# A two-layer streaming encoder on one core: products that nobody reads in three of TensorE's waits, a later wait for the latent projection's weights, and VectorE one tile further ahead

## The chip, the cores and the metric

The kernel runs on one core of one Trainium2 chip. The metric is the device time of one launch in microseconds (us), here the median of three runs. Smaller is better.

A core has TensorE (PE in the profile; its weight loads are PEld), VectorE (DVE), ScalarE (ACT), GpSimd (POOL) and a queue engine that only issues transfers (SP). Each runs its own instruction stream in order and waits for others on semaphores. Matrix products read the on-chip memory and write into PSUM, which is used here as four "pairs" of banks, `psum[0]` to `psum[3]`.

## The reference

Two layers work on 592 tokens (512 new, 16 meta, 64 sampled) of width 1024, in float32. Layer 0 mixes tokens with four recurrent heads and four attention heads, layer 1 with latent attention. Each mixer is followed by a layer norm and a mixture of 16 experts.

```python
for l in range(2):
    y = even_mixer(x) if l == 0 else odd_mixer(x)
    x = layer_norm(ALPHA * x + y)
    f = moe(x)                    # best of 4 groups, top 2 of its 4 experts, weights w
    x = layer_norm(ALPHA * x + f)

def odd_mixer(x):                 # its first steps
    cq, ckv, kpe = split(x @ w_in, [512, 768])      # 832 columns
    cq, ckv = rms_norm(cq), rms_norm(ckv)           # the latents
    kpe = rope(kpe)
    ...                           # queries, keys, values, attention, w_out

def moe(x):
    scores = sigmoid(x @ router_w)                  # 16 columns
    ...                           # choice of two experts per token
    y = sum_over_chosen(w * (silu(x @ w_gate[e]) * (x @ w_up[e])) @ w_down[e])
```

## The kernel before

**Tiles.** The tokens lie in five tiles, four of 128 and one of 80 (`TILES`, `NT = 5`). Token rows are written to memory after each norm, and transposed on TensorE into `xT` for the next product.

**Router and experts, once for each layer.** In `out_and_experts` TensorE makes the output projection of a tile (L1352), and transposes the normed tiles (`normed_tile`, L1072). After the last one it makes the router's logits (`router_logits`: L1192, then L1419). VectorE turns these into the mask of chosen experts in a chain of small operations that ends with `maskb` (L2212). TensorE then counts how many tokens choose each expert (L1366 to L1370, the "rk" product), VectorE writes one-hot rows (L2259), and TensorE reads the tokens of each slot out of them (`slot_tokens`, L1386). From these numbers GpSimd gathers the token rows of the first block of 128 slots. `experts` works through 13 such blocks. For a block TensorE transposes the rows (`rows_t`, L1434), makes gate and up (`gate_up`, L1448), transposes the hidden values (L1457) and makes the down product (`down`, L1469). After the thirteenth block every engine passes a loop over blocks that overflow (L1494 on TensorE), which are none here.

**Between the experts of layer 0 and the latents.** GpSimd gathers each token's two expert rows. On VectorE `combine_tile(i)` weights and adds them to the residual (L2408, L2410), `combined_stats(i)` takes mean and variance and subtracts the mean (L2419 to L2425), and `combined_norm(i)` scales and writes the tile (L2435). The scale itself comes from GpSimd (`scale_row`, L850 and L851). `latents(i)` (L2389 to L2399) norms and rotates what TensorE made of tile i. TensorE's loop over the tiles is: the 512 query columns of tile i (L1545), the transposes of tile i+1 (L1072), the 320 key columns of tile i (L1545), and the transposes of the latents of tile i-1 (`latents_t`, L1532 to L1535). The weights come in two items, `mi0` for the 512 columns and `mi1` for the 320. The queue issues `mi0` during the experts and `mi1` only when the first token rows have been gathered.

**What sets the order** is the code itself: each engine's program is written out by hand, and `claim`, `filled` and `wait_ge` place the waits. `weights(pe, name)` is a wait for an item's transfer. Matrix products are float32, except those on masks and one-hot rows, which are bfloat16. The code passes the identity as the operand to be loaded in some of these; `lev` is a bfloat16 constant of 1024 columns.

Of the kernel before, what the change touches and what calls it, by code (L numbers as in the profile page):

```python
# [25 lines left out]
NT = len(TILES)  # L26
# [120 lines left out]
def build_step(nc, const_where, consts, a, o):  # L147
# [11 lines left out]
    with ctx:  # L159
# [14 lines left out]
        identb = sb("identb", [128, 128], BF16)  # L174
        iotab = sb("iotab", [128, 128], BF16)

        def const(name):
            lo, hi = const_where[name]
            return cst[:, lo:hi] if lo < n_f32 else cstb[:, lo - n_f32:hi - n_f32]
# [4 lines left out]
        lev = const("lev").rearrange("p (l t) -> p l t", l=8)  # L184
# [467 lines left out]
        def weights(pe, name):  # L652

            it = next(x for x in items if x[0] == name)
            pe.wait_ge(*w_in[it[1]][name])
            return it[5]
# [409 lines left out]
        def _(pe):  # L1066
# [271 lines left out]
            def out_and_experts(l):  # L1338
# [19 lines left out]
                normed_tile(l, NT - 1)  # L1358
                router_logits(l, 1)

                pe.wait_ge(*mk_sb[l])
                ps = claim(pe, ("rk", l))
                for i in range(NT):
# [5 lines left out]
                for j in range(NT):  # L1369
                    last = pe.matmul(ps[:, 80:96], const("ones"), maskb[:, NE * j:NE * j + NE],  # L1370
                                     start=(j == 0), stop=(j == NT - 1))
                last.then_inc(pe_full.sem(("rk", l)), 1)

                slot_tokens(l, 0)
                slot_tokens(l, 1)
                pe.wait_ge(*ps_free[("rk", l)])
                pe.wait_ge(*ps_free[("lg", l, 1)])
                pe.wait_ge(*ps_free[("T", 2 * l, 4)])
                experts(l)

            def slot_tokens(l, g):
                ps = claim(pe, ("ix", l, g))
# [139 lines left out]

            out_and_experts(0)

            wq, wkv = weights(pe, "mi0"), weights(pe, "mi1")

            def latents_t(i):
                P = TILES[i]
                pe.wait_ge(*mi_sb[i])
# [4 lines left out]
                    pe.transpose(ps[:, 512 + 128 * k:512 + 128 * k + P], cvb[0:P, i % 2, 128 * k:128 * k + 128], ident[0:P, 0:P])  # L1534
                pe.transpose(ps[:, 768:768 + P], kpb[0:P, i % 2, :], ident[0:P, 0:P]).then_inc(pe_full.sem(("mt", i)), 1)  # L1535

            pe.wait_ge(*r_sb[(1, 0)])
            transpose_tile(1, 0, rb[:, 0, :])
            for i in range(NT):
                P = TILES[i]  # L1540
                pe.wait_ge(*evac[("T", 1, i)])
                ps = claim(pe, ("mi", i))
                for w, lo, n in ((wq, 0, 512), (wkv, 512, 320)):
                    for k in range(KD):
                        last = pe.matmul(ps[0:P, lo:lo + n], xT[:, k, 128 * i:128 * i + P], w[:, k, :],  # L1545
                                         start=(k == 0), stop=(k == KD - 1))
                    if lo == 0 and i + 1 < NT:
                        pe.wait_ge(*r_sb[(1, i + 1)])
                        transpose_tile(1, i + 1, rb[:, (i + 1) % 2, :])
                last.then_inc(pe_full.sem(("mi", i)), 1)  # L1550
                if i >= 1:
                    latents_t(i - 1)
# [370 lines left out]
        def _(dve):  # L1923
# [478 lines left out]
            def combine_tile(i):  # L2402

                P = TILES[i]
                acc, second = yg[0:P, i, 0, :], yg[0:P, i, 1, :]
                dve.wait_ge(*xr_in[i][(1, i, 0)])
                dve.wait_ge(*yg_in[i][0])
                stt(acc, acc, wts[0:P, 0, i:i + 1], residual(1, i)[0:P, :], ALU.mult, ALU.add).then_inc(cb_sb.sem, 1)  # L2408
                dve.wait_ge(*cb_sb[(i, "first")])
                stt(acc, second, wts[0:P, 1, i:i + 1], acc, ALU.mult, ALU.add).then_inc(cb_sb.sem, 1)  # L2410
# [34 lines left out]
            dve.wait_ge(*r_sb[(1, 0)])  # L2445
            dve.memset(pepT[64:128, 0, :], 0.0)
            dve.memset(pepT[0:64, 1, :], 0.0).then_inc(pez_sb.sem, 1)
            for i in range(NT):
                if i + 2 < NT:
                    combine_tile(i + 2)  # L2450
                if i + 1 < NT:
                    combined_norm(i + 1)
                if i + 2 < NT:
                    combined_stats(i + 2)
                latents(i)
            dve.wait_ge(*mi_sb[NT - 1])
            for i in range(NT):
# [110 lines left out]
```

## Time and profile before

| | us |
|---|---|
| median of 3 runs | 1276.92 (1275.6 to 1278.25) |
| profiled execution, device time | 1280.19 |
| its span on the core | 1277.3 |
| PE busy in the span | 1125.8 (88%) |
| DVE busy | 570.7 (45%) |
| ACT busy | 266.7 (21%) |
| POOL busy | 223.3 (17%) |

The span is the time from the first to the last instruction that the profiler saw on the core. The device time of the same execution is 2.89 us more. TensorE is the engine on which most of the chain of waits lies (77% of the span), so the reader should look for what TensorE waits for and how fast its clock runs. The column PEclk of a window is the clock that was granted to TensorE as a share of full speed: 1.00 is 2.4 GHz, 0.50 is 1.2 GHz. Over the whole span it averages 0.953.

### The profile page before, as it was taken

To read this page: it belongs to the slowest core of one execution; us is meant where nothing else is said; L and a number is where in the kernel's file an instruction comes from. 1 tells how busy PE (TensorE), PEld (TensorE's weight loads), DVE (VectorE), ACT (ScalarE), POOL (GpSimd) and SP (SyncE) were. 2 spreads that over 40 slices of the span, in tenths; PEclk is the share of its full clock that TensorE was granted. 3 is DMA by queue.
4 is the path that set the end of the run, shared out by engine and by line. 5 is a ranking of instruction groups with operands and counts; after the bars stand their busy time and mean duration, and the time that the engine had idled before them with its cause. 6 is when DMAs were issued, how large, how long until landed. Compare 5 with 4: busy or idle time off the path is not lost.

```text
span 1277.3 us, 18058 instructions
## 1 busy us (share of the span) xinstructions
PE 1125.8 (88%) x6973; PEld 632.0 (49%) x6973; DVE 570.7 (45%) x1260; ACT 266.7 (21%) x634; POOL 223.3 (17%) x382
## 2 busy tenths in 40 slices
PE   8999999999899849999749899999999975999965
PEld 4557777655654523333225446676575452333322
DVE  2079878610734435634265230450253344464226
ACT  1214334321410101111002212332331010111012
POOL 0106444321101201001052300000000211100114
PEclk9999999999999959999959999999999986999987
DMA  8113211261842468999492312000104256899935
GB/s 353 67 49 132 84 66 67 82 226 58 67 176 90 152 248 313 384 421 352 164 312 77 132 48 66 1 1 1 67 1 198 82 203 245 305 396 408 328 102 199
DMA packets 41826, 214.77 MB, mean 168 GB/s; under 512 B 4488, under 2 KB 6088, under 8 KB 32400
## 3 DMA queue, kind: packets, MB, share of 16 engines
q1 hardware_dynamic: 24288, 152.57, 30.6%
q0 software_dynamic: 17168, 60.27, 15.4%
q8 instruction: 56, 0.92, 0.3%
q10 hardware_dynamic: 288, 0.80, 0.2%
q14 instruction: 26, 0.21, 0.1%
HBM read 180.31 MB, written 33.29 MB: 167 GB/s over the span
## 4 chain that ended last, share of the span: by engine, by line
PE 77%; DVE 9%; issue 5%; DMA 5%; ACT 3%; SPq 1%; POOL 0%; DVEq 0%; ACTq 0%; POOLq 0%
PE pair L1448 12%; PE pair L1098 9%; PE pair L1352 9%; PE pair L1469 6%; PE pair L1215 5%; PE pair L1109 5%; PE pair L1281 5%; PE pair L1545 4%; PE pair L1318 3%; PE pair L1597 2%; PE pair L1086 2%; DMA arena<-x_rows,ints 2%; PE pair L1434 2%; PE pair L1139 2%; DMA ring<-in_even_w_in 2%
## 5 line engine op out<-in xcount | busy, mean ns | idle before, releaser
L1448 PE MATMUL pair<-ring,arena 128*32 128x512 f32 x608 | 128.5, 595 | 0.0
L1098 PE MATMUL pair<-ring,xT 128*128 128x512 f32 x256 | 111.3, 593 | 0.9 <-DMA ring<-in_even_w_in 0.9
L1448 PE MATMUL pair<-arena 128*32 128x512 f32 x736 | 104.8, 626 | 8.3 <-issue 4.8
L1215 PE MATMUL pair<-xT,ring 128*128 128x296 f32 x320 | 85.1, 421 | 7.0 <-ACT arena L1644 3.0
L850 POOL TENSOR_SCALAR small<-small 128x1 f32<-128x1 f32 (+3 forms) x45 | 16.9, 375 | 410.2 <-DVE small L2160 354.2
L872 POOL TENSOR_TENSOR arena<-arena 128x128 f32<-128x128 f32 x140 | 57.3, 444 | 154.2 <-PE pair L1141 86.5
L1281 PE MATMUL pair<-arena 128*128 128x264 f32 (+5 forms) x280 | 76.5, 402 | 3.3 <-ACT arena L1634 1.8
L1098 PEld LDWEIGHTS pair<-ring,xT 128*128 128x128 f32 x256 | 48.1, 190 | 59.8 <-issue 57.9
L2086 DVE TENSOR_REDUCE small<-pair 128x1 f32<-128x144 f32 (+4 forms) x40 | 22.4, 560 | 120.3 <-PE pair L1286 120.2
L1215 PEld LDWEIGHTS pair<-xT,ring 128*128 128x128 f32 x320 | 60.4, 193 | 25.8 <-issue 9.4
L998 POOL DMA_INDIRECT arena<-x_rows,ints x26 | 26.4, 1015 | 264.5 <-PE pair L1434 161.0
L2298 DVE COPY arena<-pair 128x256 f32<-128x256 f32 x26 | 11.0, 423 | 133.5 <-PE pair L1457 133.5
L1469 PE MATMUL pair<-ring,arena 128*32 128x512 f32 x304 | 65.3, 595 | 4.0 <-DVE arena L2298 4.0
L1448 PEld LDWEIGHTS pair<-arena 128*32 128x32 f32 x736 | 30.6, 115 | 68.1 <-issue 68.1
L1448 PEld LDWEIGHTS pair<-ring,arena 128*32 128x32 f32 x608 | 33.7, 110 | 57.5 <-issue 57.5
L1109 PE MATMUL pair<-arena,ring 128*128 128x296 f32 (+1 forms) x224 | 62.1, 438 | 0.0
L1545 PE MATMUL pair<-ring,xT 128*128 128x512 f32 (+3 forms) x160 | 60.0, 531 | 1.1 <-ACT xT L1626 1.1
L1352 PE MATMUL pair<-ring,mixT 128*128 128x512 f32 x128 | 57.7, 593 | 1.0 <-issue 1.0
L1352 PE MATMUL pair<-ring,xT 128*128 128x512 f32 x128 | 57.5, 592 | 0.0
L1448 PE MATMUL pair<-xT,arena 128*32 128x512 f32 x320 | 56.3, 592 | 0.0
L1626 ACT COPY xT<-pair 128x1024 f32<-128x1024 f32 (+1 forms) x15 | 14.2, 948 | 200.8 <-PE pair L1072 200.8
L1109 PEld LDWEIGHTS pair<-arena,ring 128*128 128x128 f32 x224 | 42.4, 190 | 18.1 <-issue 6.7
(366 smaller groups left out, 2022.6 us busy)
## 6 DMA issues: line engine op xcount, KB each, us to landing
arena<-in_moe_w_gate_up SPq DMA_DIRECT2D x14, 2048.0 KB
ring<-in_moe_w_gate_up SPq DMA_DIRECT2D x12, 2048.0 KB, 9.8
arena<-in_moe_w_down SPq DMA_DIRECT2D x14, 1024.0 KB
y_rows<-arena SPq DMA_DIRECT2D x26, 512.0 KB, 8.3
ring<-in_moe_w_down SPq DMA_DIRECT2D x12, 1024.0 KB, 9.5
xT<-in_moe_w_gate_up SPq DMA_DIRECT2D x6, 2048.0 KB
ring<-in_even_w_in SPq DMA_DIRECT2D x5, 2048.0 KB, 8.0
y_rows<-xr POOLq DMA_DIRECT2D x12, 512.0 KB, 8.5
```

The source lines that it names most:

```text
L872: last = pool.tensor_tensor(dst, both, mid, ALU.subtract)
L998: pool.indirect_dma_start(xg[:, e % 2, :], None, x_rows[2 * l], bass.IndirectOffsetOnAxis(ap=sloti[:, e:e + 1], axis=0)).then_inc(xg_in[e ...
L1086: last = pe.matmul(moved(ps, r, lo, n), tokens(c)[:, a:b], w[:, c, m:n], start=(c == 0), stop=(c == K - 1))
L1098: last = pe.matmul(ps[0:P, 0:n], xT[:, k, 128 * i:128 * i + P], w[:, k, :], start=(k == 0), stop=(k == chunks - 1))
L1109: last = pe.matmul(ps[0:w.shape[2], 512 * s:512 * s + n], w[:, k, :], src[:, k, n * s:n * s + n], start=(k == 0), stop=(k == chunks - 1))
L1215: last = pe.matmul(ps[0:w.shape[2], 512 * s:512 * s + n], w[:, k, :], xT[:, k, n * s:n * s + n], start=(k == 0), stop=(k == KD - 1))
L1281: last = pe.matmul(ps[0:P, lo:lo + cols], q_, k_, start=(c == 0), stop=(mask is None and c == len(lq) - 1))
L1318: last = pe.matmul(out, vb[j], pT[:, n % 2, 128 * j:128 * j + P], start=False, stop=(j == nb - 1))
L1352: last = pe.matmul(ps[0:P, 512 * half:512 * half + 512], mixed(k, i), w[:, k, :], start=(k == 0), stop=(k == KD - 1))
L1448: last = pe.matmul(bank[c, :], xgT[:, e % 2, k, c], expert_place(x)[0][:, k, :], start=(k == 0), stop=(k == KD - 1))
L1469: last = pe.matmul(psum[2][c:c + 32, 512 * half:512 * half + 512], hT[:, e % 2, 128 * k + c:128 * k + c + 32], expert_place(x)[1][:, k, 51 ...
L1545: last = pe.matmul(ps[0:P, lo:lo + n], xT[:, k, 128 * i:128 * i + P], w[:, k, :], start=(k == 0), stop=(k == KD - 1))
```

## The change

It has three parts. First, a helper `keep_busy(n)` issues n bfloat16 products of a 128x128 operand with 512 columns into `psum[1]`, whose result is read by nobody. It is called in four places in three stretches: 30 of them before the wait for the expert mask and 4 after the count, 14 before the experts start (these in both layers), and 24 before the first tile of the latent projection. Second, TensorE waits for `mi0` and `mi1` where each is used, not before the loop. Third, VectorE combines, norms and centres one tile more before it turns to the latents of a tile.

```diff
@@ out_and_experts (TensorE)
                 router_logits(l, 1)
 
+                for i in (NT - 2, NT - 1):
+                    pe.wait_ge(*ps_free[("wo", l, i)])
+                keep_busy(30)
                 pe.wait_ge(*mk_sb[l])
...
                 last.then_inc(pe_full.sem(("rk", l)), 1)
+                keep_busy(4)
 
                 slot_tokens(l, 0)
                 slot_tokens(l, 1)
...
                 pe.wait_ge(*ps_free[("T", 2 * l, 4)])
+                keep_busy(14)
                 experts(l)
+
+            def keep_busy(n):
+
+                for _ in range(n):
+                    pe.matmul(psum[1][:, 0:512], identb[:, :], const("lev")[:, 0:512], start=True, stop=True)
@@ latent projection (TensorE)
-            wq, wkv = weights(pe, "mi0"), weights(pe, "mi1")
-
...
+            pe.wait_ge(*cb_sb[(0, "first")])
+            keep_busy(24)
             pe.wait_ge(*r_sb[(1, 0)])
             transpose_tile(1, 0, rb[:, 0, :])
             for i in range(NT):
...
-                for w, lo, n in ((wq, 0, 512), (wkv, 512, 320)):
+                for name, lo, n in (("mi0", 0, 512), ("mi1", 512, 320)):
+                    w = weights(pe, name)
@@ VectorE
             dve.memset(pepT[0:64, 1, :], 0.0).then_inc(pez_sb.sem, 1)
+            combine_tile(2)
+            combined_norm(1)
+            combined_stats(2)
             for i in range(NT):
+                if i + 3 < NT:
+                    combine_tile(i + 3)
                 if i + 2 < NT:
-                    combine_tile(i + 2)
-                if i + 1 < NT:
-                    combined_norm(i + 1)
-                if i + 2 < NT:
-                    combined_stats(i + 2)
+                    combined_norm(i + 2)
+                if i + 3 < NT:
+                    combined_stats(i + 3)
                 latents(i)
```

In what follows the lines of the changed kernel are a few higher than those of before: L1419 is L1429, the count L1366 to L1370 is L1369 to L1373, L1386 is L1396, L1434 is L1444, L1448 is L1458, L1545 is L1556; on VectorE L2389 is L2400, L2408 is L2419, L2435 is L2446. `keep_busy` is L1389.

TensorE's program before, from the last logits of a layer to the first gate and up product (`maskb` is the mask, `arena` holds one-hot rows, token rows and expert weights):

```order
L1419 MATMUL pair<-cst,arena 80x16 [waits pair3_free]
L1368 MATMUL pair<-maskb,cstb 128x16 [waits pair0_free,expert_mask_written]
...
L1370 MATMUL pair<-maskb,cstb 128x16 x5
L1386 MATMUL pair<-cstb,arena 128x2 [waits onehots_written,pair3_free]
...
L1434 MATMUL pair<-cst,arena 128x128 [waits pair2_free,expert_rows_loaded0,pair3_free,pair0_free]
L1434 MATMUL pair<-cst,arena 128x128 x7
```

The same place in the changed kernel:

```order
L1429 MATMUL pair<-cst,arena 80x16 [waits pair3_free]
L1389 MATMUL pair<-cstb,identb 128x512 [waits pair1_free,pair0_free]
L1389 MATMUL pair<-cstb,identb 128x512 x29
L1371 MATMUL pair<-maskb,cstb 128x16 [waits pair0_free,expert_mask_written]
...
L1373 MATMUL pair<-maskb,cstb 128x16 x5
L1389 MATMUL pair<-cstb,identb 128x512 x4
L1396 MATMUL pair<-cstb,arena 128x2 [waits onehots_written,pair3_free]
...
L1389 MATMUL pair<-cstb,identb 128x512 [waits pair2_free,pair3_free,pair0_free]
L1389 MATMUL pair<-cstb,identb 128x512 x13
L1444 MATMUL pair<-cst,arena 128x128 [waits expert_rows_loaded0]
```

The three batches stand between instructions whose own waits are the ones they had; the waits for free PSUM pairs have moved to the head of a batch.

TensorE's program before at the latent projection, from the end of layer 0's overflow loop:

```order
L1494 COMPARE_AND_BRANCH
L1072 MATMUL pair<-cst,rb 128x128 [waits ln_written,pair2_free,weights_loaded2,weights_loaded0]
L1072 MATMUL pair<-cst,rb 128x128 x7
L1545 MATMUL pair<-ring,xT 128x512 [waits pair1_free,pair2_free]
L1545 MATMUL pair<-ring,xT 128x512 x7
L1072 MATMUL pair<-cst,rb 128x128 [waits pair2_free,ln_written]
L1072 MATMUL pair<-cst,rb 128x128 x7
L1545 MATMUL pair<-ring,xT 128x320 x8
```

In the changed kernel the batch of 24 and the products of tile 0 read:

```order
L1389 MATMUL pair<-cstb,identb 128x512 [waits token_rows_combined]
L1389 MATMUL pair<-cstb,identb 128x512 x23
L1556 MATMUL pair<-ring,xT 128x512 [waits weights_loaded0,pair1_free,pair2_free]
L1556 MATMUL pair<-ring,xT 128x512 x7
...
L1556 MATMUL pair<-ring,xT 128x320 [waits weights_loaded2]
L1556 MATMUL pair<-ring,xT 128x320 x7
```

The wait for `mi1` (`weights_loaded2`) has gone from the first transposes to the first 320-column product, behind the first eight query products and the transposes of tile 1.

VectorE's program before, around the latents of tiles 0 and 1. L2435 writes a normed tile (tiles 1 and 2 here), L2389 is the first instruction of a tile's latents:

```order
L2435 SCALAR_TENSOR_TENSOR rb<-arena,small,lng 128x1024 [waits token_rows_combined,ln_scale_ready,pair2_full,rows_stored1]
...
L2389 SCALAR_TENSOR_TENSOR arena<-pair,small,arena 128x512 [waits mla_rms_ready,mla_gains_loaded,pair1_full]
...
L2410 SCALAR_TENSOR_TENSOR arena<-arena,small 128x1024 [waits token_rows_combined]
L2435 SCALAR_TENSOR_TENSOR rb<-arena,small,lng 128x1024 [waits token_rows_combined,ln_scale_ready,pair2_full,rows_stored0]
...
L2389 SCALAR_TENSOR_TENSOR arena<-pair,small,arena 128x512 [waits mla_latents_written,mla_rms_ready,pair0_full]
```

And in the changed kernel:

```order
L2446 SCALAR_TENSOR_TENSOR rb<-arena,small,lng 128x1024 [waits token_rows_combined,ln_scale_ready,pair2_full,rows_stored1]
...
L2421 SCALAR_TENSOR_TENSOR arena<-arena,small 128x1024 [waits token_rows_combined]
L2446 SCALAR_TENSOR_TENSOR rb<-arena,small,lng 128x1024 [waits token_rows_combined,ln_scale_ready,pair2_full,rows_stored0]
...
L2400 SCALAR_TENSOR_TENSOR arena<-pair,small,arena 128x512 [waits mla_rms_ready,mla_gains_loaded,pair1_full]
...
L2446 SCALAR_TENSOR_TENSOR rb<-arena,small,lng 128x1024 [waits token_rows_combined,ln_scale_ready,pair2_full,rows_stored1]
...
L2400 SCALAR_TENSOR_TENSOR arena<-pair,small,arena 128x512 [waits mla_latents_written,mla_rms_ready,pair0_full]
```

Tile 2's norm now stands ahead of tile 0's latents, and tile 3's norm ahead of tile 1's.

## Rows read from the trace of the kernel before

**Rows 1.** Waits of TensorE, whole span: total us, times, longest.

```profile
PE pair L1072 <- DMA ring<-in_mla_w_in: 24.2, 1, 24.2
PE pair L1368 <- DVE maskb L2212: 18.8, 2, 9.4
PE pair L1434 <- DMA arena<-x_rows,ints: 10.8, 4, 3.8
PE pair L1448 <- issue: 4.8, 2, 2.5
...
PE pair L1072 <- DVE rb L2435: 1.8, 2, 1.3
```

**Rows 2.** Stretches: start:end, length, busy us by engine (instructions), PEclk, DMA share, GB/s.

```profile
446.40:473.50 27.10, 9.18 (x85) 4.79 (x82) 12.43 (x53) 1.08 (x3) 3.13 (x3) 0.50 0.76 303
...
1040.00:1047.00 7.00, 3.78 (x33) 2.01 (x32) 5.64 (x10) 1.60 (x2) 2.16 (x3) 1.00 0.98 384
1047.10:1074.20 27.10, 8.56 (x81) 4.79 (x85) 12.43 (x53) 1.73 (x4) 3.20 (x3) 0.50 0.80 318
...
637.50:664.60 27.10, 7.20 (x14) 3.73 (x15) 20.07 (x24) 1.01 (x1) 19.43 (x20) 0.50 0.98 332
```

**Rows 3.** TensorE in order of time, layer 0: start, us, instruction, idle before it.

```profile
447.30 0.45 PE L1419 MATMUL pair<-cst,arena 128*80 128x16 f32 x2 [0.33 <-ACT arena L1803]
457.16 0.20 PE L1368 MATMUL pair<-maskb,cstb 128*128 128x16 bf16 x1 [9.41 <-DVE maskb L2212]
...
461.96 0.29 PE L1386 MATMUL pair<-cstb,arena 128*128 128x2 bf16 x5 [0.44 <-DVE arena L2259]
466.00 1.94 PE L1434 MATMUL pair<-cst,arena 128*128 128x128 f32 x8 [3.76 <-DMA arena<-x_rows,ints]
468.82 9.41 PE L1448 MATMUL pair<-arena 128*32 128x512 f32 x64 [0.87 <-DVE arena L2278]
478.16 1.09 PE L1434 MATMUL pair<-cst,arena 128*128 128x128 f32 x8
```

**Rows 4.** TensorE's bfloat16 products by shape: count, busy, mean ns.

```profile
L1286 PE MATMUL pair<-cstb,identb 80*80 80x512 bf16 x12 | 4.6, 381 | 0.0
...
L1286 PE MATMUL pair<-cstb,identb 128*128 128x128 bf16 x16 | 3.5, 219 | 0.0
```

**Rows 5.** The chain that ended last, in order of time: start, us, what.

```profile
505.76 6.87 PE pair L1448 x64
...
645.19 11.02 DMA ring<-in_mla_w_in
656.30 1.95 PE pair L1072 x8
...
659.34 9.79 PE pair L1545 x16
...
702.17 6.87 PE pair L1545 x16
...
1070.33 9.04 PE pair L1448 x64
...
1182.29 8.77 PE pair L1448 x64
...
1236.07 9.87 issue
```

**Rows 6.** VectorE in order of time, between the experts and the latents.

```profile
643.15 1.28 DVE L2408 SCALAR_TENSOR_TENSOR arena<-arena,small,xr 128x1024 f32<-128x1024 f32 x1 [1.48 <-DMA arena<-y_rows,ints]
...
651.07 1.28 DVE L2435 SCALAR_TENSOR_TENSOR rb<-arena,small,lng 128x1024 f32<-128x1024 f32 x1
...
658.70 1.28 DVE L2435 SCALAR_TENSOR_TENSOR rb<-arena,small,lng 128x1024 f32<-128x1024 f32 x1
...
661.46 1.28 DVE L2425 SCALAR_TENSOR_TENSOR arena<-arena,small,lng 128x1024 f32<-128x1024 f32 x1
676.65 0.75 DVE L2389 SCALAR_TENSOR_TENSOR arena<-pair,small,arena 128x512 f32<-128x512 f32 x1 [13.91 <-POOL small L851]
```

## The prediction

> **What bounds the kernel now.** I read the waits of TensorE first, then the granted clock by stretch, then the order of time around each. TensorE waits longest in one piece for `mi1`, 24.2 us, then twice 9.4 for the expert mask [rows 1]. Each of these is followed by a stretch at PEclk 0.50, that is 1.2 GHz: 446.4 to 473.5, 637.5 to 664.6 and 1047.1 to 1074.2 [rows 2]. So each wait is paid twice, once as time and once in products at half the clock. Neither long wait can vanish: the mask and the combined rows come from VectorE. What can go is the slow clock after them, and the part of the 24.2 that is owed to `mi1` alone.
>
> What counts is how much dense work TensorE did before the clock rose. The first gate and up began at 468.82 and the clock stood at 1.00 from about 473.5: 4.7 us. In layer 1 it was 1070.33 to 1074.3, 4.0 us, and at the latents 659.34 to 664.7, 5.4 us [rows 2, 3, 5]. I take 5 us, and 4 to 6 as bounds.
>
> **What one unread product costs.** It has its own rows: a bfloat16 product of `cstb` and `identb` takes 381 ns with 512 columns and 219 with 128 [rows 4]. The difference, 162 ns for 384 columns, is 0.42 ns a column, so in a row of equal ones each costs 512 x 0.42 = 0.216 us at 2.4 GHz and twice that, 0.43, at 1.2. The 381 ns contain a start and end that overlap with the neighbour; an upper bound is thus 0.38. A batch of n that begins at the low clock costs 5 us for its first 11.6 products and 0.216 for each of the rest: 30 cost 5 + 4.0 = 9.0 us (8.5 to 9.4 by the bounds of the rise, 12.9 if the clock never rises), 24 cost 7.7 (7.2 to 8.2, never: 10.3).
>
> **The 30 before the mask.** TensorE is free at 447.75 and the mask releases it at 457.16, 9.4 us later [rows 3]. The waits for the output projection's PSUM add nothing, as VectorE has read that before the last transposes. The batch ends at 456.7 (456.2 to 457.2): cost 0, hidden by VectorE's router chain. Queued behind it is the count, for which VectorE waits, so any overrun is on the path one to one; never rising would cost 12.9 - 9.4 = 3.5 us.
>
> **The 4 after the count** take 0.9 us (1.7 at the low clock) beside VectorE's one-hot rows, whose wait is of that size. Cost 0.
>
> **The 14 before the experts.** They start at 462.25, after the last slot product, and the gathered rows release the transposes at 466.00 [rows 3]: 3.75 us of cover. At 2.4 GHz they take 3.0, cost 0. But from the count to this point TensorE has only the 4 and some narrow products in over 4 us, and the clock may have fallen. Then they take 5 us for 11.6 and 0.5 for the rest, 5.5 us or at worst 6.0, and the transposes start 1.8 to 2.2 late. I put the term at +1.2, with 0 and 2.2 as ends: nearer to the fall, since in 1040 to 1047 the clock fell with TensorE busy for 3.78 of 7.00 us [rows 2].
>
> The Trainium skill (TensorE: Matmul & The Clock Gate, Part 4: PE-mode transpose) says that a transpose is not counted as activity in the way other products are. The trace agrees as far as it goes: that stretch of 1040 to 1047 held transposes and narrow logits, and the clock fell after it. By that rule the eight transposes and the pauses after a batch are as good as idle, and the time would be the second rival's 1266.3 at least; without it, it is the forecast.
>
> **What a warm clock gives.** In both cases the clock is high when the experts begin. The transposes take 1.09 us, as for the second block, instead of 1.94, so 0.9 less [rows 3]. Gate and up take 6.87 as in the later blocks [rows 5] instead of 9.41 in layer 0 (2.5 less) and 9.04 in layer 1 (2.2 less) [rows 3, 5]. With +1.2 for the late 14: layer 0 gains 0.9 + 2.5 - 1.2 = 2.2, layer 1 gains 0.9 + 2.2 - 1.2 = 1.9. Together 4.1 (2.1 to 6.5). What is late next are the gathers and weights of later blocks. Their transfers are released by TensorE's own products, so they should move forward with it.
>
> **The latents.** Three edits act together. VectorE ends the first combine at 643.15 + 1.28 = 644.43 and tile 0's norm at 651.07 + 1.28 = 652.35 [rows 6]. TensorE must have left the overflow loop by 644.43. In layer 1 that took 9.87 us of issue after 1236.07 [rows 5]; in layer 0 TensorE's last product ended 24.2 us before 656.30 [rows 1, 5], at 632.1, so with some 0.7 us for the copies behind it the loop ends near 642.7, just in time. The 24 take 7.7 us, 644.5 to 652.2 (651.7 to 652.7, never rising 654.8). So the transposes of tile 0 start at 652.5, not at 656.30, which was when `mi1` had landed: 645.19 + 11.02 = 656.21 [rows 5]. They take 1.09 and not 1.95. ScalarE's copy and its signals took from 658.25 to 659.34, 1.1 us, and stay. The query products start at 652.5 + 1.1 + 1.1 = 654.7 instead of 659.34: 4.6 gained. They take 6.87 instead of 9.79 [rows 5]: 2.9 more. The next transposes want tile 1's norm (659.98 [rows 6]) at 661.5, which is there, and `mi1` is wanted at 662.6, 6 us after it lands. So moving its wait costs nothing.
>
> From there VectorE's order matters. Before, tile 2's norm stood behind tile 0's latents, and TensorE waited 1.8 us in two pieces, for tiles 2 and 3 [rows 1]. VectorE was idle for 13.91 us between tile 2's statistics (end 662.7) and those latents [rows 6], so tile 3's combine (2 x 1.28 less some overlap, 2.5 us), tile 2's norm (1.2) and tile 3's statistics and centring (2.8) fit into it: 662.7 to 669.2. Tile 2's norm is there at 666.4 and is wanted at about 674. The 320-column products take 6.87 x 320/512 = 4.3. Before, tile 0's products ended at 659.34 + 9.79 + 0.9 + 4.3 = 674.3, and its latents began at 676.65, 2.4 later (ScalarE's squares and GpSimd's root). Now they end at 654.7 + 6.9 + 1.1 + 4.3 = 667.0 and the latents can begin at 669.4: VectorE is just free. Tile 3's norm now stands between the latents of tiles 0 and 1 and needs GpSimd's scale, which GpSimd makes only after it has stored tile 0's latents; it is wanted near 687, 15 us after those latents, which is ample. The 1.8 us go entirely. GpSimd's queue moves with it: the second gather, the stores and tile 4's residual keep their order, and the queue's wait for tile 3's combine ends earlier.
>
> Sum here: 4.6 + 2.9 + 1.8 = 9.3 us. Bounds: 0.5 less for a late end of the 24; nothing more to gain but 0.2.
>
> **Sum and conversion.** 9.3 + 4.1 = 13.4 less. The sum is on a span of 1277.3 and a device time of 1280.19 in the profiled execution, which would become 1266.8. That execution is 3.3 us (0.26%) above the median of the runs, 1276.92. I subtract from the median: 1263.5.
>
> Some slow stretches will fall otherwise than now, in either direction. At 1182.29 a gate and up took 8.77 instead of 6.87 [rows 5] right after one of the two waits without a releaser [rows 1]. One such stretch is worth 1.9 us, and I allow for one or two either way.
>
> **Rivals.**
> *The experts give it back.* TensorE waited 4.8 us in two pieces at a gate and up for no instruction, probably for weights in flight [rows 1]. If these land at a time set by bandwidth alone, a start 2 us earlier only lengthens those waits. For: the two waits name no instruction and stand where weights are due. Against: the transfers start when TensorE has used the place they go to, so they move forward too. Price: the 4.1, time 1276.9 - 9.3 = 1267.6.
> *The clock falls again in the short pauses.* After the 24 come 1.04 us of transposes and 1.1 of waiting; after the 14 much the same. For: 1040 to 1047 [rows 2]. Against: the later blocks have the same pauses between them and ran at 6.87 [rows 5]. If the clock falls at tile 0, the query products take 9.79 again, 2.9 us; if also at one layer's experts, 2.2 to 2.5 more. Time 1266.3 to 1268.8.
> *The unread products do not raise the clock.* They stay at 0.43 us. Then the 30 overrun by 3.5 us and the 14 take 6.0 against 3.75 of cover, 2.2 more, twice, with no gain behind: +11.4. The 24 end at 654.8, still 1.5 before 656.30, and the norms' 1.8 stay: -3.3. Time 1276.9 + 8.1 = 1285.0, slower. It decides from the point at which the 30 cost over 9.4 us. Against it: every dense stretch in [rows 2] was followed by a rise.
> *Nothing changes*, since the norm and the mask set the pace: within 0.2%, 2.6 us. Against: the 9.79 and 9.41 lie in the chain itself.
>
> **Numbers.** Forecast 62%, experts give it back 12%, clock falls again 16%, slower 5%, nothing 3%, and 2% for more than the sum. The predicted time is 1263.5. The range from 1258.5 (all bounds and one or two slow stretches gone) to 1269.5 takes in the two rivals of the same sign. A change under 0.2% would not be told from none: faster 0.92, same 0.03, slower 0.05.
>
> **What would show it.** The products of `keep_busy` at about 0.43 us each and later 0.22; PEclk at 1.00 before the mask and from the first expert transposes on; first gate and up near 6.9 us in both layers; no wait for `mi1` at all; tile 0's transposes no longer released by a transfer and beginning 3.8 us earlier against the end of the experts; no wait for L2446 at tiles 2 and 3. It is wrong if the count starts later than the mask by over 1 us, if the experts' transposes are late and slow, or if the waits without a releaser at gate and up grow by 2 us.

## The result and the profile after

| | before | changed |
|---|---|---|
| median, 15 runs each | 1280.67 us (1275.6 to 1286.29) | 1270.82 us (1266.88 to 1278.27) |
| profiled execution, device time | 1280.19 | 1270.41 |
| its span | 1277.3 | 1268.6 |
| PE busy | 1125.8 | 1154.7 |

The ratio is 0.9922, with a 95% interval of 0.9905 to 0.9939: 10 us faster, between 7.8 and 12.2. I had forecast 13.4 us less, as 1263.5, with a range from 1258.5 to 1269.5. The direction was right and the time lies outside the range. The three runs of before from which I subtracted had a median of 1276.92; fifteen give 1280.67.

TensorE's waits in the changed kernel (total us, times, longest), which answer to [rows 1]:

```profile
PE pair L1389 <- DVE arena L2419: 12.6, 1, 12.6
...
PE pair L1458 <- issue: 4.6, 2, 2.6
PE pair L1444 <- DMA arena<-x_rows,ints: 4.6, 2, 2.3
...
PE pair L1371 <- DVE maskb L2223: 2.9, 2, 1.8
```

The 24.2 for `mi1` and the 1.8 for the norms of tiles 2 and 3 are gone. Of the 24.2 the 12.6 up to the first combine are left, and the batch of 24 stands in the rest. The 18.8 for the mask have become 2.9. The 10.8 for gathered rows are 4.6, and these are no longer at the first block.

TensorE's busy time and granted clock by stretch in layer 0 (start:end, length, busy us by engine, PEclk, DMA share, GB/s), which answer to [rows 2]:

```profile
444.30:450.90 6.60, 4.50 (x31) 2.70 (x33) 2.49 (x9) 1.19 (x3) 0.60 (x1) 0.50 1.00 413
451.10:461.00 9.90, 6.96 (x53) 3.17 (x51) 7.70 (x37) 0.00 (x0) 0.00 (x0) 1.00 1.02 432
461.20:467.90 6.70, 5.30 (x22) 2.14 (x23) 2.10 (x8) 0.00 (x0) 2.20 (x2) 0.50 0.69 223
468.10:502.00 33.90, 29.81 (x281) 12.07 (x280) 12.73 (x25) 3.49 (x7) 2.98 (x3) 1.00 0.63 234
502.30:505.40 3.10, 3.10 (x18) 0.78 (x20) 2.72 (x4) 0.58 (x1) 0.00 (x0) 0.50 0.98 421
```

The one slow stretch of 27.1 us in [rows 2] has become three, of 6.8, 6.8 and 3.4 us. The clock rises during the batch of 30, falls again at 461 before the batch of 14, and falls a third time at 502, where nothing fell before. Here is the same place in TensorE's order of time (start, us, instruction, idle before), against [rows 3]:

```profile
448.27 0.45 PE L1429 MATMUL pair<-cst,arena 128*80 128x16 f32 x2 [0.34 <-ACT arena L1814]
448.93 7.40 PE L1389 MATMUL pair<-cstb,identb 128*128 128x512 bf16 x29 [0.22 <-issue]
458.12 0.18 PE L1371 MATMUL pair<-maskb,cstb 128*128 128x16 bf16 x1 [1.79 <-DVE maskb L2223]
...
462.87 0.29 PE L1396 MATMUL pair<-cstb,arena 128*128 128x2 bf16 x5 [0.44 <-DVE arena L2270]
463.03 5.61 PE L1389 MATMUL pair<-cstb,identb 128*128 128x512 bf16 x14
468.47 1.04 PE L1444 MATMUL pair<-cst,arena 128*128 128x128 f32 x8
470.38 7.07 PE L1458 MATMUL pair<-arena 128*32 128x512 f32 x64 [0.88 <-DVE arena L2289]
477.39 1.09 PE L1444 MATMUL pair<-cst,arena 128*128 128x128 f32 x8
...
501.31 1.26 PE L1444 MATMUL pair<-cst,arena 128*128 128x128 f32 x8 [2.34 <-DMA arena<-x_rows,ints]
...
514.92 1.04 PE L1444 MATMUL pair<-cst,arena 128*128 128x128 f32 x8
```

Each block begins with eight transposes, so the rows of L1444 count the blocks: the first four begin at 468.47, 477.39, 486.88 and 501.31.

The batch of 14 took 5.61 us. The transposes of the first block start 10.35 us after the mask, against 8.84 in [rows 3]; the second block's start 19.27 after it, against 21.00. So 1.5 us were lost and 3.2 won. In layer 1 the 14 took 4.66 us. At 501.31 the fourth block waits 2.34 us for its rows. In layer 1 the same place reads

```profile
1092.72 1.97 PE L1444 MATMUL pair<-cst,arena 128*128 128x128 f32 x8 [2.28 <-DMA arena<-x_rows,ints]
```

with its eight transposes at the slow clock, 1.97 us instead of 1.09. In layer 0 of the kernel before, the fourth and fifth blocks begin at

```profile
501.10 1.09 PE L1434 MATMUL pair<-cst,arena 128*128 128x128 f32 x8 [1.36 <-DMA arena<-x_rows,ints]
...
513.08 1.04 PE L1434 MATMUL pair<-cst,arena 128*128 128x128 f32 x8
```

From one to the other it takes 11.98 us there and 13.61 in the changed kernel (13.52 in its layer 1). So a fall of the clock at this place costs 1.6 us.

The start of the latents in TensorE's order of time, against [rows 5]:

```profile
646.64 7.92 PE L1389 MATMUL pair<-cstb,identb 128*128 128x512 bf16 x23 [12.60 <-DVE arena L2419]
654.40 1.04 PE L1072 MATMUL pair<-cst,rb 128*128 128x128 f32 x8
656.54 7.13 PE L1556 MATMUL pair<-ring,xT 128*128 128x512 f32 x16 [1.10 <-ACT xT L1637]
```

I compare the two profiles by stages, each from an event of its own, so that what went before is out of it. Two rows of a trace subtracted give each number.

| stage | before | changed | difference |
|---|---|---|---|
| start to the first mask | 457.16 | 458.12 | +0.96 |
| mask to the last product of the experts, layer 0 | 174.91 | 175.93 | +1.02 |
| from there to the last product of the latents' tile 4 | 93.82 | 84.15 | -9.67 |
| from there to the second mask | 332.87 | 332.35 | -0.52 |
| mask to the last product of the experts, layer 1 | 176.65 | 175.90 | -0.75 |
| from there to the end | 41.89 | 42.15 | +0.26 |

The sum is the 8.7 us between the spans. Practically all of it is in the latents. The two expert stages, for which I had counted -4.1, give +0.3.

### The profile page after: what moved, and what is told of

It reads as the page before. It is cut to its first block, busy times and chain, and to the rows that moved or that the text cites. A ratio compares the mean times of both kernels' runs of the same rounds, so it can differ in the third digit from the quotient of the medians.

```text
span 1268.6 us, 18292 instructions
## 1 busy us (share of the span) xinstructions
PE 1154.7 (91%) x7088; PEld 644.2 (51%) x7093; DVE 572.9 (45%) x1260; ACT 266.3 (21%) x634; POOL 221.7 (17%) x382
## 4 chain that ended last, share of the span: by engine, by line
PE 80%; DVE 9%; issue 4%; DMA 3%; ACT 3%; POOL 0%; DVEq 0%; ACTq 0%; POOLq 0%; SPq 0%
PE pair L1458 12%; PE pair L1098 9%; PE pair L1352 9%; PE pair L1479 6%; PE pair L1281 5%; PE pair L1109 5%; PE pair L1215 4%; PE pair L1556 4%; PE pair L1318 3%; PE pair L1608 2%; PE pair L1086 2%; PE pair L1444 2%; PE pair L1588 2%; PE pair L1139 2%; PE pair L1316 2%
## 5 line engine op out<-in xcount | busy, mean ns | idle before, releaser
L1458 PE MATMUL pair<-ring,arena 128*32 128x512 f32 x608 | 128.5, 595 | 0.0
L1458 PE MATMUL pair<-arena 128*32 128x512 f32 x736 | 100.5, 600 | 8.1 <-issue 4.6
L872 POOL TENSOR_TENSOR arena<-arena 128x128 f32<-128x128 f32 x140 | 56.6, 438 | 153.5 <-PE pair L1141 85.5
L1458 PEld LDWEIGHTS pair<-ring,arena 128*32 128x32 f32 x608 | 33.7, 110 | 57.8 <-issue 57.8
L1458 PEld LDWEIGHTS pair<-arena 128*32 128x32 f32 x736 | 30.4, 111 | 63.5 <-issue 63.5
L1556 PE MATMUL pair<-ring,xT 128*128 128x512 f32 (+3 forms) x160 | 57.3, 513 | 1.1 <-ACT xT L1637 1.1
L1458 PE MATMUL pair<-xT,arena 128*32 128x512 f32 x320 | 56.3, 592 | 0.0
L1479 PE MATMUL pair<-arena 128*32 128x512 f32 x368 | 53.0, 608 | 0.0
```

The lines of the kernel that those rows point to most:

```text
L872: last = pool.tensor_tensor(dst, both, mid, ALU.subtract)
L1458: last = pe.matmul(bank[c, :], xgT[:, e % 2, k, c], expert_place(x)[0][:, k, :], start=(k == 0), stop=(k == KD - 1))
L1479: last = pe.matmul(psum[2][c:c + 32, 512 * half:512 * half + 512], hT[:, e % 2, 128 * k + c:128 * k + c + 32], expert_place(x)[1][:, k, 51 ...
```

## The experiments

Times are ratios to the kernel before in the same comparison, with 95% intervals. One microsecond is 0.08%. The profile of each was read by the same stages. Most intervals reach 0.2% to either side, so the stages are the sharper instrument.

| kernel | ratio | 95% |
|---|---|---|
| the changed kernel | 0.9922 | 0.9905 to 0.9939 |
| e1 without 30, 4 and 14 | 0.9927 | 0.9907 to 0.9946 |
| e2 only 30, 4 and 14 | 0.9975 | 0.9956 to 0.9995 |
| e3 without the 14 | 0.9924 | 0.9905 to 0.9942 |
| e4 with 8 at the third block | 0.9903 | 0.9876 to 0.9930 |
| e5 VectorE's old order | 0.9928 | 0.9906 to 0.9951 |
| e6 without the 24 | 0.9909 | 0.9888 to 0.9930 |
| e7 weight wait ahead of the 24 | 0.9989 | 0.9973 to 1.0005 |
| e8 with 6 between the slot products | 0.9884 | 0.9862 to 0.9906 |
| e10 weight wait behind the 24 | 0.9969 | 0.9953 to 0.9985 |
| e11 60 instead of 30 | 0.9987 | 0.9970 to 1.0004 |
| e12 e4 and e8 together | 0.9870 | 0.9842 to 0.9898 |
| e13 e12 and three more fills | 0.9836 | 0.9808 to 0.9863 |

### Which part gives the time: e1 and e2

```diff
# e1: the changed kernel, in both layers
-                for i in (NT - 2, NT - 1):
-                    pe.wait_ge(*ps_free[("wo", l, i)])
-                keep_busy(30)
...
-                keep_busy(4)
...
-                keep_busy(14)
```

> The changed kernel without the batches of 30, 4 and 14 in either layer; the 24, the late wait for mi1 and VectorE's order stay. Theory A (the latents give the whole gain, the router's products give nothing on balance): 9 to 10 us under the kernel before, ratio 0.992 to 0.993, and no gain at all in the experts. Theory B (both give, as I predicted, and the latents give less than I read): 5 to 6 us under it, ratio near 0.9955. In the trace, from the last product of layer 0's experts to the last 320-column product of tile 4: 94 us before, 84.5 by A.

Measured: 0.9927, 9.3 us under the kernel before. From the end of the experts to the end of the latents it took 85.47 us, 8.4 less than before. e2 is the counterpart:

```diff
# e2: the changed kernel
-            pe.wait_ge(*cb_sb[(0, "first")])
-            keep_busy(24)
...
+                for w, lo, n in ((wq, 0, 512), (wkv, 512, 320)):
# and VectorE's loop as in the kernel before
```

> The kernel before with only the batches of 30, 4 and 14 in both layers. Theory A: within 1.5 us of the kernel before, ratio 0.999 to 1.001; the first gate and up takes 7.07 us instead of 9.4, but its transposes start 1 to 2 us later after the mask, and the gather of the third block's rows takes the rest: TensorE waits 2.3 us for it in both layers. Theory B: 4 us under it, ratio 0.997.

Measured: 0.9975, 3.2 us under it, but with an interval from 0.6 to 5.6, in which both theories lie. The stage of the experts took 175.41 and 173.62. What this and the later expectations call the third block, the one that waits for its gather, is the fourth; I had miscounted. It waited for its rows 1.03 us in one layer and 1.17 in the other. TensorE in order of time in e2:

```profile
500.44 1.09 PE L1444 MATMUL pair<-cst,arena 128*128 128x128 f32 x8 [1.03 <-DMA arena<-x_rows,ints]
...
1102.04 1.09 PE L1444 MATMUL pair<-cst,arena 128*128 128x128 f32 x8 [1.17 <-DMA arena<-x_rows,ints]
```

No slow stretch follows these waits, where one follows the 2.34 us of the changed kernel.

What follows: the latents carry nearly the whole gain, which is theory A. That the router's part gives nothing, as A said, is not shown: e2 gives it 0.6 to 5.6 us, and e1 against the changed kernel 0.6 us, well inside the intervals.

### Is the late batch of 14 worth having: e3

```diff
-                keep_busy(14)
                 experts(l)
```

> The changed kernel without the two batches of 14. Theory C (the 14 meet a fallen clock, run 5.6 us and make the transposes 1.5 us late, but raise the clock for the first gate and up): the transposes start 8.8 us after the mask as before, and both they and the first gate and up are slow again, 1.94 and about 9.4; against the changed kernel 1.5 us given back and 3.4 lost per layer, so 3 to 4 us above the changed kernel. Rival D (the clock stays up over the pause because of the 30 and 4, the 14 are only in the way): transposes 1.04 at 8.8 us after the mask and gate and up 6.9 to 7.1, 3 us under the changed kernel.

TensorE in order of time in e3, first block of layer 0:

```profile
466.26 1.94 PE L1443 MATMUL pair<-cst,arena 128*128 128x128 f32 x8 [4.43 <-DMA arena<-x_rows,ints]
469.07 9.38 PE L1457 MATMUL pair<-arena 128*32 128x512 f32 x64 [0.88 <-DVE arena L2288]
```

The clock had fallen without the 14, and transposes and gate and up were as slow as in [rows 3]. That is theory C; D falls. In the profiles the fourth block started 45.1 and 45.0 us after the mask, against 43.2 and 42.2 with the batch. The ratio, 0.9924, does not show the 3 to 4 us that C expected, so what the 14 are worth in time stays open. What the trace shows is that the clock raised by the 30 is lost again before the experts begin.

### Does the fourth block's wait cost a second fall: e4

```diff
                     if e + 1 < NX:
+                        if e == 1:
+                            keep_busy(8)
                         rows_t(l, e + 1)
```

> The changed kernel with 8 more unread products ahead of the transposes of the third block, in the wait for its gathered rows (1.7 us at 2.4 GHz). Theory E (the clock falls at 502 and 1092 us because of this wait of 2.3 us): PEclk stays 1.00 there in both layers, 3 us under the changed kernel. Rival F (the falls are chance, at places that move from run to run): no difference beyond 1 us, and other falls in their stead.

TensorE in order of time in e4:

```profile
486.69 1.67 PE L1389 MATMUL pair<-cstb,identb 128*128 128x512 bf16 x7
488.20 1.04 PE L1444 MATMUL pair<-cst,arena 128*128 128x128 f32 x8
...
500.47 1.09 PE L1444 MATMUL pair<-cst,arena 128*128 128x128 f32 x8 [0.18 <-DMA arena<-x_rows,ints]
```

This is not the test that the expectation describes. The 8 stand ahead of the third block's transposes, where TensorE had no wait at all, and the wait for the gather comes one block later. So they did not fill the wait. They pushed TensorE back by 1.7 us, and the fourth block's wait shrank from 2.34 and 2.28 us to 0.18 and 0.76. The clock did not fall there in either layer. That agrees with theory E, in that a shorter wait brought no fall, but whether products inside the wait would do it was not tried. The clock fell at the tenth block in both layers (580.6 and 1174.5), for 3.4 us. The second of these falls is in the changed kernel too, also at 1174.5, and e2 has one there in both layers, so they are not the price of this edit. The ratio moved from 0.9922 to 0.9903, inside the intervals; a gain is not shown by this run.

### The three edits of the latents: e5, e6, e7 and e10

```diff
# e5: VectorE, from the changed kernel back to the order of before
-            combine_tile(2)
-            combined_norm(1)
-            combined_stats(2)
             for i in range(NT):
-                if i + 3 < NT:
-                    combine_tile(i + 3)
+                if i + 2 < NT:
+                    combine_tile(i + 2)
...
```

> The changed kernel with VectorE's old order (tile i+2's combine and tile i+1's norm ahead of tile i's latents). By my sum the order is worth 1.8 us: TensorE waits again 1.3 and 0.5 us for the norms of tiles 2 and 3, or more, since the products before them now come earlier. Theory G (the order is needed for the rest): TensorE reaches tile 2's transposes with the old distance behind tile 0's latents, so the waits are the old 1.8 and the kernel is 1.8 us above the changed one. Rival H (the order is worthless): no wait over 0.3 us, time as the changed kernel.

TensorE's waits from 600 to 740 us in e5:

```profile
PE pair L1072 <- DVE rb L2446: 2.7, 3, 1.3
```

Theory G: three waits, 2.7 us in all. Two of them, 1.30 and 0.49 us for the norms of tiles 2 and 3, are the 1.8 us of the sum. The third, 0.86 us for the norm of tile 0, is in e1 and e4 as well, with 1.20 and 0.89. The stage took 87.94 us. In kernels with the same slow stretch at 655 (e1, e4) it took 85.47 and 85.75, so the order is worth 2.2 to 2.5 us. The ratio of 0.9928 alone would not have told it.

```diff
# e6: the changed kernel
-            pe.wait_ge(*cb_sb[(0, "first")])
-            keep_busy(24)
             pe.wait_ge(*r_sb[(1, 0)])
```

> The changed kernel without the 24. By my sum: the transposes start as early (some 20.3 us after the last product of the experts), but at 1.2 GHz: 0.9 more for them and 2.9 more for the first query products, 3.8 us above the changed kernel. Rival (the clock would fall again in the pauses anyway): under 1 us above it.

The stage took 86.41 us, 2.3 more than the changed kernel in its profile, 0.9 more than e1 and 0.7 more than e4. The transposes started as early, 20.22 us after the experts, and the first query products took 8.60 us. TensorE in order of time in e6:

```profile
661.41 8.60 PE L1554 MATMUL pair<-ring,xT 128*128 128x512 f32 x16 [1.10 <-ACT xT L1635]
```

The clock rose early in them by itself. With the 24 they took 7.13 in the changed kernel, but 8.57 in e1 and 8.83 in e4 and e5, where the batch ended some 1 us before tile 0's norm was there and the clock fell once more just behind it. So the 24 are worth 0.7 to 2.3 us in these profiles and not my 3.8, and the ratio, 0.9909, shows no worth at all.

```diff
# e7: both weight waits ahead of the batch
+            wq, wkv = weights(pe, "mi0"), weights(pe, "mi1")
...
             pe.wait_ge(*cb_sb[(0, "first")])
             keep_busy(24)
# e10: the same line, but between keep_busy(24) and the wait for r_sb
```

> The changed kernel with both weight waits ahead of the loop again, behind the 24. By my sum: the transposes of tile 0 start when mi1 has landed, 24 us after the last product of the experts and not 20.3, so 3.7 us above the changed kernel, and with 2 us of pause ahead of them the clock may fall again, 3 us more. Rival (mi1 lands earlier, the wait was not for it): no difference.

> The changed kernel with both weight waits between the 24 and the wait for tile 0's norm (in e7 they stood ahead of the 24 and held these back as well). By my sum: the transposes start when mi1 has landed, 24 us after the last product of layer 0's experts instead of 20.3, so the latents end 3.7 us later than in the changed kernel, or 6.6 if the clock falls in the 2 to 4 us pause behind the 24. Rival (the 24 alone bring the gain, the later weight wait nothing): the latents end as in the changed kernel.

In e7 I had put the line ahead of the batch, not behind it as its expectation says. So the 24 themselves waited for `mi1`, as TensorE's row in e7 shows (start, us, instruction, idle before):

```profile
656.75 6.32 PE L1389 MATMUL pair<-cstb,identb 128*128 128x512 bf16 x23 [23.85 <-DMA ring<-in_mla_w_in]
```

The transposes then started 30.00 us after the experts. That is 9.65 later than in the changed kernel, and the ratio is 0.9989. By e10, below, 3.6 us of this are the wait for `mi1`. The other 6.0 are what the batch costs when it stands behind a wait and not in it. At the end of the stage less of it is left (93.8 us against e10's 91.3), since the transposes and query products behind the batch ran at 2.4 GHz. e10 is the test meant. Its waits of TensorE in 600 to 740 us:

```profile
PE pair L1072 <- DMA ring<-in_mla_w_in: 4.9, 1, 4.9
```

The transposes started 23.99 us after the experts, 3.6 later than in the changed kernel, and the clock fell in the pause of 4.9 us: the stage took 91.27, which is 7.1 more. The ratio is 0.9969, 6 us above the changed kernel. So the late weight wait is the largest single part: 3.6 by itself and 3.5 through the clock (the transposes took 1.94 us and the query products 9.71).

### Why the experts gave so little: e8

```diff
                 slot_tokens(l, 0)
+                keep_busy(6)
                 slot_tokens(l, 1)
```

> The changed kernel with 6 more unread products between the first two slot products (1.3 us at 2.4 GHz, cover 1.5). Theory I (the clock falls at 461 and 1055 us because TensorE has only narrow products between the count and the 14): with these 6 the clock stays up in at least one layer, the 14 take 3.0 us and the experts' transposes start 8.8 us after the mask and not 9.4 to 10.7, 1 to 3 us under the changed kernel. Rival J (too few to hold it): the clock falls as before, the 6 take 2.6 us at the low clock and delay VectorE by 1 us a layer, 2 us above the changed kernel.

Clock and busy time by stretch in e8, both layers:

```profile
450.50:466.00 15.50, 11.66 (x82) 5.10 (x80) 9.61 (x42) 0.00 (x0) 2.19 (x2) 1.00 0.92 365
466.00:500.00 34.00, 30.48 (x288) 12.41 (x292) 13.28 (x26) 4.05 (x8) 2.99 (x3) 1.00 0.65 241
500.00:634.00 134.00, 124.20 (x1144) 43.18 (x1136) 61.64 (x131) 16.19 (x32) 11.26 (x15) 1.00 0.88 335
1040.90:1056.00 15.10, 11.68 (x82) 5.14 (x81) 9.56 (x41) 0.00 (x0) 2.26 (x2) 1.00 0.88 348
1056.00:1224.00 168.00, 154.48 (x1428) 55.25 (x1428) 74.91 (x156) 22.01 (x45) 14.81 (x18) 1.00 0.80 306
```

and TensorE in order of time:

```profile
462.01 3.18 PE L1390 MATMUL pair<-cstb,identb 128*128 128x512 bf16 x14
466.44 1.09 PE L1445 MATMUL pair<-cst,arena 128*128 128x128 f32 x8 [1.25 <-DMA arena<-x_rows,ints]
468.51 7.07 PE L1459 MATMUL pair<-arena 128*32 128x512 f32 x64 [0.97 <-DVE arena L2290]
```

Theory I: the clock stayed at 2.4 GHz in both layers, the 14 took 3.18 us, and the gather ends the wait again, not the batch. From the mask to the end of the experts it took 172.58 and 172.77 us, 3.3 and 3.1 less than the changed kernel, and no slow stretch stood in either stage. The ratio of 0.9884 is 4.9 us under the changed kernel's. A single stage would not prove it: e6's layer 1, without the 6, took 172.75 too. But the six layers with the 6 (e8, e12, e13) average 172.7, and the twelve with only the 30, 4 and 14 (the changed kernel, e2, e5, e6, e7, e10) 175.4.

The later falls are tied to the 14. A batch that begins at 1.2 GHz ends just behind the rise, so the fourth block follows that rise at a nearly fixed distance: in the changed kernel 33 us, from 468.0 to 501.3, and 34 us in layer 1. There the clock fell in all nine profiled layers with the batches cold at their start and 1.9 us or more of wait for the gather (the changed kernel, e5, e7 and e10 in both layers, e6 in layer 0), and in none of four with less (e2 twice, e6 and e11 once each). e11's layer 0, with 2.40, makes a tenth. Where the 14 were left out (before, e1 and e3), six layers waited 1.4 to 2.6 us there and none fell; nor did e8 and e12 in their layer 1, where the 14 began at 2.4 GHz and the wait was 2.47 and 2.56. So the length of the wait alone does not decide. Why a pause of 2.3 us is harmless in one kernel and not in the other stays open; that it is the distance from the rise is an inference from these rows, and no run moved it by itself.

### The price of a product, and more fills: e11, e12 and e13

```diff
-                keep_busy(30)
+                keep_busy(60)
```

> The changed kernel with 60 unread products before the mask instead of 30. By my sum each of the further 30 costs 0.216 us at the high clock, 6.5 us; the wait for the mask has 1.1 to 1.8 us left, so the count starts 4.7 to 5.4 us late in each layer, and the kernel is 10 us above the changed one, near the kernel before. Rival (the products are cheaper in a row, or the wait is not on the path): under 4 us above it.

The first counting product of layer 0 in e11, from TensorE's order of time:

```profile
461.56 0.17 PE L1371 MATMUL pair<-maskb,cstb 128*128 128x16 bf16 x1
```

The 60 began at 447.61 and took 14.12 us. VectorE had written the mask at 457.11, so the count stood 4.4 us late, at 461.56; in layer 1 the 60 took 14.92 and the count was 5.2 us late. The ratio rose from 0.9922 to 0.9987, 8.3 us. The queue behind a batch pays for it one to one, as the sum had it.

e12 is the changed kernel with the edits of e4 and e8. e13 adds this, with `keep_busy(n, pair)` writing to a free pair:

```diff
                 last.then_inc(pe_full.sem(("pt", j)), 1)
+                if j < 3:
+                    pe.wait_ge(*ps_free[("mi", 3)])
+                    keep_busy((8, 3, 3)[j], 0)
```

> The changed kernel with both the 6 between the slot products and the 8 ahead of the third block's transposes. Theory K (each stops a fall of its own): 3.5 us under the changed kernel for the 6, and 1 us more for the 8 where the clock would have fallen at the third block. Rival L (where the 6 keep the clock up at the first block, the third needs nothing): as with the 6 alone, and the 8 only take from the cover, within 1 us.

> The kernel of e12 with 8, 3 and 3 unread products in the three pauses between the transposes of the old latents (2.0, 0.9 and 0.9 us), where the clock fell for 3.4 to 6.9 us in all runs so far. Theory: the clock stays up there and 1.7 to 2.6 us go, some 2 us under e12. Rival (they are still too thin, or overrun ScalarE's copies): no gain, or 0.5 us more.

e12 gives 0.9870 and e13 0.9836. In e12's profile the experts had no slow stretch, as in e8 alone, so the 8 are not shown to add to the 6. The 1.8 us between the two ratios lie inside the intervals, and K and L are not told apart. As in e4, the 8 stand one block ahead of the wait, and e12's fourth block still waited 2.56 us in layer 1. In e13 TensorE's order of time just behind the latents reads, around one of the new fills,

```profile
715.70 1.89 PE L1390 MATMUL pair<-cstb,identb 128*128 128x512 bf16 x8
717.90 0.55 PE L1571 MATMUL pair<-cst,arena 128*128 128x128 f32 x3 [0.31 <-ACT arena L1896]
...
721.17 7.03 PE L1594 MATMUL pair<-mixT,arena 128*128 128x512 f32 x16
```

and the following products took 7.03 us, where the changed kernel's took 8.27 and e12's 8.39. The fall of the clock that e12 has at 719 is gone, the one at 739 stayed, and the stage up to the second mask took 330.9 us against 332.4. That is 1.5 us, a little under the 1.7 to 2.6 expected. The ratios of e12 and e13 lie 4.4 us apart, and their intervals overlap. e13 is the best version: 21 us under the kernel before and 11 under the changed one.

## Why the prediction was wrong, point by point

**The latents.** Right in place and in sum: 9.3 forecast, 9.67 in the profile, 9.3 for e1. Some of the agreement is luck. In the changed kernel's profile the clock stayed up behind the 24. In e1, e4 and e8 it fell once more there, as the second rival had it, and the stage took 85.5 to 85.8 us, 8.1 to 8.4 less than before. Why it fell there and not in e12, with as long a wait for tile 0's norm (1.25 us), stays open. Inside the sum the shares were off. The wait for `mi1` was right (3.6, with e10). VectorE's order saved the 1.8 us of waits as forecast, and 2.2 to 2.5 in the stage. The 24 were worth 0.7 to 2.3 and not 3.8. My error there was to take the cold 9.79 of [rows 5] as what the query products cost without a batch. That price was for products that began 4 us later; begun earlier, they took 8.60 without any batch. The parts overlap, so they do not add up to the whole.

**The price of a product, the 30 and the 4.** The price was right: in e8, 6 products at 2.4 GHz took 1.46 us and 14 took 3.18, so each further one costs 0.215. How long dense work runs before the clock rises was not. I took 5 us with bounds of 4 and 6. In the changed kernel the clock rose 2.0 and 3.5 us after the 30 began, 4.9 and 3.0 us after the 14 began, and 5.6 us after the 24 began. So 29 took 7.40 us in one layer and 8.14 in the other, against my 9.0 and bounds from 8.5. The mask's wait covered them, and e11 showed the price beyond the cover.

**The 14 before the experts, the step that failed in mechanism.** I had the fall of the clock before them as likely, and priced it at +1.2 us a layer; in the changed kernel's profile the transposes were 1.5 and 0.6 late. The gain on the first gate and up was right too: 7.07 instead of 9.4. What I missed is what comes after. I wrote that the later blocks' transfers are released by TensorE's own products and move forward with it. They did: in layer 0 GpSimd issued the fourth block's gather 34.2 us after the mask instead of 35.9, though its rows then took 9.0 us to land instead of 8.0. Over the twelve layers with only these batches (the changed kernel, e2, e5, e6, e7 and e10) the fourth block started 42.6 us after the mask, against 44.4 in the four without (before and e1), which is 1.8 of my 2.1. Its wait for the gather was no longer than in those four (1.0 to 2.4 us against 1.4 to 2.6). But in nine of the twelve the clock fell there, at 1.6 us each, and in none of the four. My sum had no fall at this place. The end of the stage kept only 0.7 (175.4 against 176.1 us), in layers that lie between 172.8 and 178.6. So the term "what a warm clock gives", 4.1, measured 0.6 as e1 against the changed kernel and 3.2 as e2 against before. Both fit a value of about 2, and 4.1 less two falls of 1.6 would be 0.9. A smaller slip is in this term and in the latents: my 6.87 is from products right behind others, and behind a wait they took 7.07 at the experts and 7.13 at the latents. That made each of the three gains 0.2 to 0.3 us too large.

**The rival "the experts give it back"** had the right outcome in the profile and the wrong cause. The waits without a releaser stayed at 4.6 us. It is the second rival's mechanism, the clock that falls in short pauses, which took the gain. The rival had it at the first block and at tile 0; it came before the 14, at the fourth block, and at tile 0 in some profiles. e8 supports it: six products, in a pause that covers them, keep the clock up through both stages, and the kernel is 4.9 us under the changed one, though the two intervals just touch.

**Sum and conversion, the step that put the time out of the range.** I subtracted 13.4 from the median of three runs. Over 15 runs of before the median was 3.75 us higher, and in later comparisons it was 1281 to 1282. Against that base my sum gives 1267.3, inside the range, and the measured change of 10 us is three quarters of the forecast. My profiled execution, 1280.19, was already 3.3 above the three, and I had noted it and set it aside. The range came from the terms and had nothing for the base.

**The slower rival** (products that do not raise the clock) fell: the clock rose in every batch of 30.

## What to carry to other kernels

A batch of unread products that raises the clock is worth little unless the stretch up to the real work is filled as well; look for the thinnest pause behind it, and fill that first. Put the batch inside the wait and not behind it (6.0 us of delay in e7), and bound its size by the shortest cover, since the queue behind it pays at once. And read a stage from an event of its own before adding up: the median of three runs was off by more than a third of the whole effect.

## What the runs showed of the hardware

With the 14 begun at 1.2 GHz, and no further batch in the experts, the clock fell at the same place, the fourth block's transposes, in ten of fourteen layers. The ten had waited 1.9 to 2.4 us for the gather and the other four 1.0 to 1.4. It fell not once in the six layers without the 14, though five of them waited 2.0 to 2.6 us. Each of these falls cost 1.6 us up to the next block. Products that nobody reads raise the clock like any others: in the changed kernel it rose in both batches of 30 before they ended, 7.40 and 8.14 us long. Programs on this one core also spread more than my forecast allowed for: 15 runs of the same kernel lie between 1275.6 and 1286.29 us, 0.8%. Not tried: unread products in the fourth block's own wait, the down product of the second block put ahead of the fourth block's transposes, which would have moved that pause away from the clock's rise, and whether fewer than 24 or 30 would do as well in the kernels of e8 to e13.
